# Issuing each head pair's scores behind another pair's probability product, and moving the forget gate's sum to GpSimd, in a hybrid decoder block

## Chip, cores and metric

The kernel runs on one core of a Trainium2 chip, as one launch. The metric is the device time of that launch in microseconds (us). The time before is the median of three runs.

## What is computed

The program is one decoder block on x of 512 tokens by 1024 channels, in float32:

```python
xn = rms_norm(h, norm_mix_w)
hq, hf, hi, hg, fq, fk, fv, ff, ga, gb = split(xn @ w_in)
a = hgrn2_mixer(hq, hf, hi, hg, lb)      # 4 heads of 128
b = fox_attention(fq, fk, fv, ff, fb)    # 8 heads of 64
h = h + (sigmoid(ga) * (a @ w_a) + sigmoid(gb) * (b @ w_b)) @ w_out
h = h + peer_ffn(rms_norm(h))            # 16384 experts, 128 slots a token
return rms_norm(h)
```

The change touches `fox_attention` and its order beside the rest. For each head it computes

```python
log_f = log_sigmoid(ff + fb)             # ff: 512 tokens x 8 heads
c = cumsum(log_f, axis=token)
s[t, u] = q[t] . k[u] / 8 + c[t] - c[u]  # u <= t
o = softmax(s) @ v
```

The softmax does not depend on c[t], so the kernel adds only -c[u].

## The kernel before

The launch has three stages, separated by barriers. The first, which the change touches, ends at about 386 us of the profiled span: the input projection, the HGRN2 mixer and the attention. The second has the branch, output and query projections, and the third (most of the time) the experts.

**Weights as units.** Every weight matrix is cut into units of 1024x128. A unit is loaded by a DMA of SyncE's queue (`load_unit`), split by ScalarE into a rounded high part (`split_hi`, L210) and by GpSimd into the remainder (`split_lo`, L214), and used by TensorE in 24 matmuls (`unit_product` and `passes`, L219 to L221: high by high, high by low, low by high). Splits run four units ahead of their use (`LEAD`), and loads seven (`LOAD_LEAD`).

**The order in stage one.** Each of the five engines runs a loop over the same steps n = 0 to 44, one unit of `w_in` each: forget logits of HGRN2 at 0 to 3, its queries at 4 to 7, its values at 8 to 11, the attention's values at 12 to 15, the attention's forget logits `ff` at 16 (`FF0`), its queries at 17 to 20, its keys at 21 to 24, the merge gates at 25 to 40 and the HGRN2 output gates at 41 to 44. In each step TensorE first projects the unit (`project(n)`) and then issues what that step holds of the mixers. VectorE and ScalarE take their part of the same step in program order. Which mixer work lies in which step is written out by hand:

- HGRN2 is 4 heads of 11 events, two events a step, from `HG_STEP0` = 9 on. Events 0 to 6 of a head are levels: VectorE takes differences (`pre1`), ScalarE the exponential (`hgrn_exp`), VectorE multiplies (`pre2`, L545 and L546), TensorE multiplies (`hgrn_mm`, L714), VectorE selects (`post`, L568). Event 7 is the diagonal (L718). Event 8, OFFX, has six ScalarE instructions (L396 to L401), six on VectorE (L552 to L557) and then the matmuls of L723. Event 10 is the output (L730 to L737). VectorE does `pre2` of the second event of a step inside that step.
- The attention has 4 head pairs p, each in three steps from `FX_STEP0` = 31 on. At 31+3p TensorE issues the scores (`fox_scores_mm`, L754 to L762), VectorE takes row maxima (L584), ScalarE the exponentials (`act_fox_exp`, L365) and VectorE normalizes (L592, both in `fox_norm`). At 32+3p TensorE transposes the probabilities (`fox_transposes`, L773) and ScalarE copies them out (`act_fox_trout`, L375 and L379). At 33+3p TensorE multiplies by the values into bank 7 (`fox_pv`, L783), which VectorE copies out (`fox_out`, L597) at the head of its step 34+3p. The last of a pair's eight score blocks, head 1 by query tile 1, is in bank 7 too.
- `ON_STEP` sets where the HGRN2 output norm of each head goes (ScalarE L473, TensorE L798, VectorE L655); ScalarE takes the roots of all four at step 36 (L477), and VectorE the reciprocal and scaling of each head at steps 38, 39, 41 and 42 (`ROW_STEP`, L665 and L666).
- The forget sum is VectorE's, on 8 partitions. At step 16: bias (L622), absolute value (L625), minimum with zero (L627), negation (L628). ScalarE takes exponential and logarithm at step 17 (L453 and L455). At step 18 VectorE subtracts (L631), fills ones (L632) and scans (L633). At steps 20, 22 and 24 (`C_STEPS`) it peels off one of three bfloat16 parts of the sum into rows 0, 32 and 64 of `negc3` (L637 to L639) and writes the rows of `head_row` that select a head (L641, 8 instructions). Pair 0's scores wait for all of it.

## Time and profile before

| | before |
|---|---|
| median of three runs (1795.12, 1801.9, 1802.53) | 1801.9 us |
| the profiled execution | 1790.98 us |
| its span | 1789.2 us |
| mean granted TensorE clock | 0.986 of full speed |
| TensorE busy | 1721.5 us, 96% |
| VectorE busy | 1231.1 us, 69% |
| ScalarE busy | 778.7 us, 44% |
| GpSimd busy | 776.5 us, 43% |

The span is the stretch between the first and the last instruction of one profiled execution. The engines overlap, so their busy times do not add up to it. Idle time is given in the profile in front of the instruction that ended it, with the instruction that released it.

### The profile page before, as it was taken

The page shows a single profiled execution, that of the slowest core. Times are in us where ns is not written, and L with a number is a line of the kernel's source. Part 1 is how long each engine was busy: PE and PEld are TensorE (multiplying, and loading weights), DVE is VectorE, ACT ScalarE, POOL GpSimd, SP SyncE. Part 2 cuts the span into 40 slices and gives each one's busy share as a digit, 9 for nine tenths or more (in the row PEclk, how much of TensorE's full clock was granted, in tenths as well). Part 3 has the DMA queues.
Part 4 walks back from the last instruction along what each step waited for, and adds up shares of the span by engine and source line. Part 5 has one row for each costly group of instructions (what it writes and reads, how often), then busy time and mean ns, then how long its engine had stood idle before and what let it go on. Part 6 is the DMA issues. An engine that isn't in the chain of part 4 may idle for free.

```text
span 1789.2 us, 25724 instructions
## 1 busy us (share of the span) xinstructions
PE 1721.5 (96%) x9603; PEld 1603.3 (90%) x9603; DVE 1231.1 (69%) x2306; ACT 778.7 (44%) x1367; POOL 776.5 (43%) x478
## 2 busy tenths in 40 slices
PE   6998999989999999999999999998999999999996
PEld 4786876668788999999999999998999999999996
DVE  6556633464252589999989866643888888888884
ACT  4333325444321333346677766733333333333332
POOL 4332322234333487876554567784232223232210
PEclk8999999999999999999999999999999999999998
DMA  6332232235433599987777799998999999999981
GB/s 172 92 83 56 69 107 83 77 121 168 115 114 107 179 312 298 323 303 277 251 277 254 283 321 361 376 376 319 350 350 350 363 357 351 344 371 336 356 304 48
DMA packets 260844, 436.09 MB, mean 244 GB/s; under 512 B 14960, under 2 KB 184176, under 8 KB 259056
## 3 DMA queue, kind: packets, MB, share of 16 engines
q1 hardware_dynamic: 203696, 249.87, 43.2%
q0 software_dynamic: 36864, 134.23, 19.8%
q10 hardware_dynamic: 20160, 50.34, 7.5%
q8 instruction: 77, 1.26, 0.3%
q14 instruction: 47, 0.39, 0.1%
HBM read 373.57 MB, written 60.82 MB: 243 GB/s over the span
## 4 chain that ended last, share of the span: by engine, by line
PE 47%; issue 6%; DVE 5%; POOL 5%; DMA 3%; ACT 1%; SPq 0%; DVEq 0%; POOLq 0%; ACTq 0%
PE bank L219 13%; PE bank L221 13%; PE bank L220 13%; PE x_rows L219 2%; PE x_rows L221 2%; PE x_rows L220 2%; POOL rows L1081 2%; POOL spl_a L214 2%; PE bank L1531 1%; DMA rows<-in_u_rows,expert 1%; DVE rows L1090 1%; DMA raw<-in_v_tab 1%; DMA raw<-in_u_t 1%; DVE hot L1316 0%; DVE lists L1344 0%
## 5 line engine op out<-in xcount | busy, mean ns | idle before, releaser
L214 POOL TENSOR_TENSOR spl_a<-raw,spl_a 128x1024 fp32r<-128x1024 f32 x172 | 413.5, 2406 | 394.0 <-ACT spl_a L210 393.1
L210 ACT ACTIVATE spl_a<-raw 128x1024 fp32r<-128x1024 f32 x296 | 312.9, 1059 | 401.4 <-PE bank L221 280.6
L219 PE MATMUL bank<-act,spl_a 128*128 128x384 f32 (+1 forms) x1216 | 431.3, 355 | 12.1 <-DVE act L509 7.4
L220 PE MATMUL bank<-act,spl_a 128*128 128x384 f32 (+1 forms) x1216 | 420.1, 345 | 0.0
L221 PE MATMUL bank<-act,spl_a 128*128 128x384 f32 (+1 forms) x1216 | 420.0, 345 | 0.0
L1081 POOL DMA_INDIRECT rows<-in_v_tab,expert x128 | 142.2, 1111 | 352.6 <-DVE hot L1457 339.5
L219 PE MATMUL bank<-aws,spl_a 128*128 128x384 f32 x768 | 258.3, 336 | 5.9 <-POOL spl_a L214 5.9
L220 PE MATMUL bank<-aws,spl_a 128*128 128x384 f32 x768 | 258.1, 336 | 0.0
L221 PE MATMUL bank<-aws,spl_a 128*128 128x384 f32 x768 | 258.0, 336 | 0.0
L219 PEld LDWEIGHTS bank<-act,spl_a 128*128 128x128 f32 x1216 | 230.6, 190 | 26.1 <-issue 13.7
L220 PEld LDWEIGHTS bank<-act,spl_a 128*128 128x128 f32 x1216 | 231.1, 190 | 8.5 <-issue 1.7
L221 PEld LDWEIGHTS bank<-act,spl_a 128*128 128x128 f32 x1216 | 230.3, 189 | 8.2
L214 DVE TENSOR_TENSOR spl_a<-raw,spl_a 128x1024 fp32r<-128x1024 f32 x124 | 151.9, 1225 | 96.4 <-ACT spl_a L210 96.4
L1090 DVE SCALAR_TENSOR_TENSOR rows<-rows,x_rows 128x1024 f32<-128x1024 f32 x128 | 155.0, 1215 | 76.6 <-DMA rows<-in_u_rows,expert 76.3
L1231 ACT ACTIVATE aws<-scb 128x384 fp32r<-128x384 f32 x128 | 67.2, 525 | 224.9 <-DVE scb L1438 224.5
L214 POOL TENSOR_TENSOR spl_b<-raw,spl_b 128x1024 fp32r<-128x1024 f32 x37 | 90.2, 2441 | 164.3 <-ACT spl_b L210 164.3
L1457 DVE SCALAR_TENSOR_TENSOR hot<-rows,a_row,hot 128x1024 f32<-128x1024 f32 x126 | 160.7, 1279 | 0.0
L219 PEld LDWEIGHTS bank<-aws,spl_a 128*128 128x128 f32 x768 | 144.7, 188 | 6.2 <-POOL spl_a L214 6.2
L220 PEld LDWEIGHTS bank<-aws,spl_a 128*128 128x128 f32 x768 | 144.8, 188 | 0.0
L221 PEld LDWEIGHTS bank<-aws,spl_a 128*128 128x128 f32 x768 | 144.8, 188 | 0.0
L1081 POOL DMA_INDIRECT rows<-in_u_rows,expert x128 | 123.2, 962 | 30.5 <-issue 16.5
L1266 ACT ACTIVATE hot<-hot,slot_t 128x128 f32<-128x128 f32 x384 | 119.6, 397 | 14.0 <-DVE hot L1316 11.6
(294 smaller groups left out, 2814.4 us busy)
## 6 DMA issues: line engine op xcount, KB each, us to landing
raw<-in_u_t SPq DMA_DIRECT2D x128, 512.0 KB, 4.6
raw<-in_v_tab SPq DMA_DIRECT2D x128, 512.0 KB, 8.5
gelu_ux<-gl ACTq DMA_DIRECT2D x128, 192.0 KB, 4.9
dense_gates<-mixbuf ACTq DMA_DIRECT2D x12, 2048.0 KB, 9.0
mixbuf<-dense_gates SPq DMA_DIRECT2D x32, 768.0 KB, 9.1
mixbuf<-gelu_ux SPq DMA_DIRECT2D x32, 768.0 KB, 12.2
raw<-in_w_in SPq DMA_DIRECT2D x45, 512.0 KB, 3.9
raw<-in_w_q SPq DMA_DIRECT2D x16, 512.0 KB, 3.9
```

The source lines that it names most:

```text
L210: eng.activation(spl(n, 0, slice(0, W)), raw[:, s, :], ACT.Copy).then_inc(hi_done, 1)
L214: eng.tensor_tensor(spl(n, 1, slice(0, W)), raw[:, n % RAW, :], spl(n, 0, slice(0, W)).bitcast(F32), ALU.subtract).then_inc(lo_done, 1)
L219: nc.tensor.matmul(out, w_hi, x_hi, start=first, stop=False)
L220: nc.tensor.matmul(out, w_hi, x_lo, start=False, stop=False)
L221: return nc.tensor.matmul(out, w_lo, x_hi, start=False, stop=last)
L1081: pool.indirect_dma_start(out=rows[:, g % ROWS, :], out_offset=None, in_=u_rows[:, :] if g < SLOTS else v_rows, in_offset=bass.IndirectOff ...
L1090: dve.scalar_tensor_tensor(out=row, in0=row, scalar=1.0, in1=x, op0=ALU.mult, op1=ALU.mult, accum_out=z_row[:, g:g + 1]).then_inc(row_used, 1)
L1231: act_e.activation(aws[:, 0, j % AWS, :], aw[:, j % 2, :], ACT.Copy).then_inc(a_hi, 1)
L1266: ins = act_e.activation(hot[:, q % HOTS, 1, t, :], hot[:, q % HOTS, 1, t, :], ACT.Copy, scale=slot_t[:, 2, col:col + 1])
L1457: dve.scalar_tensor_tensor(out=acc[:, s % 2, :], in0=row, scalar=a_row[:, s:s + 1], in1=acc[:, s % 2, :], op0=ALU.mult, op1=ALU.add) \
L1531: ins = nc.tensor.matmul(bank[4 + q % 2][:, t * P:(t + 1) * P], hot[:, q % HOTS, 0, t, :], hot[:, q % HOTS, 1, t, :], start=True, stop=True)
```

## The change

The HGRN2 events and the attention's steps go one step later. The scores of pairs 1, 2 and 3 are issued at steps 34, 37 and 40, the step of the previous pair's value product and right behind it; transposes are at 33, 36, 39, 42 and value products at 34, 37, 40, 43. VectorE copies a pair's product out in the product's own step, ahead of the next pair's `fox_norm`. On TensorE the wait for that copy stands only before the last of the eight blocks. The root goes to step 35, and the four scalings to 36, 36, 39 and 39.

The `ff` unit comes from a new array `w_ff`, in which the 8 columns stand three times (rows 0, 32, 64 of the result, zeros between), so the sum is made on 72 partitions. VectorE keeps the bias (step 16) and the scan (step 21). GpSimd makes the rest behind its own splits: three instructions at step 17, two at step 19, six and a no-operation at step 21, most of them followed by a wait for their own end (`link`). ScalarE's exponential and logarithm go to step 18. `head_row` comes from a new input of 72x1024 float32 (`c_head`, 295 KB) by a DMA ahead of the first unit's load and one GpSimd copy, in place of 24 VectorE copies; two GpSimd fills go.

```diff
-HG_STEP0 = 9
-FX_STEP0 = 31
+HG_STEP0 = 10
+FX_STEP0 = 32
-ROW_STEP = [38, 39, 41, 42]
-C_STEPS = [20, 22, 24]
+ROOT_STEP = 35
+ROW_STEP = [36, 36, 39, 39]
+SCORES_STEP = [FX_STEP0] + [FX_STEP0 + 3 * p - 1 for p in range(1, PAIRS_FX)]
...
                 sp.dma_start(probs[:, 0:8 * P], c_mask).then_inc(mask_in, 16)
+                sp.dma_start(probs_t[0:FR, 0:HF * P], c_head).then_inc(mask_in, 16)
...
-                pool.wait_ge(mask_in, 16)
+                pool.wait_ge(mask_in, 32)
...
+                pool.tensor_copy(head_row[:, :, :].rearrange("p h t -> p (h t)"), probs_t[0:FR, 0:HF * P]) \
+                    .then_inc(c_ready, 1)
...
                 for n in range(N_IN):
                     split_lo(pool, n + LEAD)
+                    if n == FF0 + 1:
+                        pool.wait_ge(proj_out[FF0 % 2], FF0 // 2 + 1)
+                        link(pool.tensor_scalar(negc[:, :], ff[:, 0, :], 0.0, None, ALU.min))
+                        link(pool.tensor_tensor(ff[:, 1, :], negc[:, :], ff[:, 0, :], ALU.subtract))
+                        pool.tensor_tensor(ff[:, 1, :], ff[:, 1, :], negc[:, :], ALU.add).then_inc(ff_abs, 1)
+                    if n == FF0 + 3:
+                        pool.wait_ge(ff_soft, 1)
+                        link(pool.tensor_tensor(ff[:, 0, :], negc[:, :], ff[:, 1, :], ALU.subtract))
+                        pool.memset(ff[:, 1, :], 1.0).then_inc(ff_log, 1)
+                    if n == FF0 + 5:
+                        pool.wait_ge(lo_done, n + LEAD + 1)
+                        pool.wait_ge(ff_scan, 1)
+                        link(pool.tensor_copy(negc3[:, :], negc[:, :]))
+                        link(pool.tensor_tensor(negc[:, :], negc[:, :], negc3[:, :], ALU.subtract))
+                        link(pool.tensor_copy(negc3[32:64, :], negc[32:64, :]))
+                        link(pool.tensor_copy(negc3[64:FR, :], negc[64:FR, :]))
+                        link(pool.tensor_tensor(negc[64:FR, :], negc[64:FR, :], negc3[64:FR, :], ALU.subtract))
+                        link(pool.tensor_copy(negc3[64:FR, :], negc[64:FR, :]))
+                        pool.nop(nofuse=True).then_inc(c_ready, 1)
...
                     if n == FF0:
                         dve.wait_ge(unit_used, n + 1)
-                        dve.tensor_scalar(ff[:, 0, :], pr[0:HF, :], fbias[:, 0:1], None, ALU.add) \
+                        dve.tensor_scalar(ff[:, 0, :], pr[0:FR, :], fbias[:, 0:1], None, ALU.add) \
                             .then_inc(proj_out[n % 2], 1)
-                        dve.wait_ge(proj_out[n % 2], n // 2 + 1)
-                        dve.scalar_tensor_tensor(out=ff[:, 1, :], in0=ff[:, 0, :], scalar=-1.0,
-                                                 in1=ff[:, 0, :], op0=ALU.mult, op1=ALU.max)
-                        link(dve.tensor_scalar(negc[:, :], ff[:, 0, :], 0.0, None, ALU.min))
-                        dve.tensor_scalar(ff[:, 1, :], ff[:, 1, :], -1.0, None, ALU.mult).then_inc(ff_abs, 1)
-                    if n == FF0 + 2:
-                        dve.wait_ge(ff_soft, 1)
-                        link(dve.tensor_tensor(ff[:, 0, :], negc[:, :], ff[:, 1, :], ALU.subtract))
-                        link(dve.memset(ff[:, 1, :], 1.0))
-                        link(dve.tensor_tensor_scan(negc[:, :], ff[:, 1, :], ff[:, 0, :], 0.0,
-                                                    ALU.mult, ALU.subtract))
-                    if n in C_STEPS:
...
+                    if n == FF0 + 5:
+                        dve.wait_ge(ff_log, 1)
+                        dve.tensor_tensor_scan(negc[:, :], ff[:, 1, :], ff[:, 0, :], 0.0,
+                                               ALU.mult, ALU.subtract).then_inc(ff_scan, 1)
...
-                    if part == 0 and 0 < p <= PAIRS_FX:
-                        fox_out(p - 1)
-                    if part == 0 and 0 <= p < PAIRS_FX:
-                        fox_norm(p)
+                    if part == 2 and 0 <= p < PAIRS_FX:
+                        fox_out(p)
+                    if n in SCORES_STEP:
+                        fox_norm(SCORES_STEP.index(n))
...
                     else:
                         pe.wait_ge(fx_trout, 6 * p)
-                        pe.wait_ge(fx_out, p)
                     for a in range(2):
                         for i in (3, 2, 0, 1):
+                            if p and (a, i) == (1, 1):
+                                pe.wait_ge(fx_out, p)
...
-                    if 0 <= p < PAIRS_FX:
-                        [fox_scores_mm, fox_transposes, fox_pv][part](p)
+                    if part == 1 and 0 <= p < PAIRS_FX:
+                        fox_transposes(p)
+                    if part == 2 and 0 <= p < PAIRS_FX:
+                        fox_pv(p)
+                    if n in SCORES_STEP:
+                        fox_scores_mm(SCORES_STEP.index(n))
```

## Rows read from the trace of the kernel before

**Rows 1.** The page: TensorE's busy time, and its granted clock in 40 slices.
```profile
PE 1721.5 (96%) x9603; PEld 1603.3 (90%) x9603; DVE 1231.1 (69%) x2306; ACT 778.7 (44%) x1367; POOL 776.5 (43%) x478
...
PEclk8999999999999999999999999999999999999998
```

**Rows 2.** TensorE's waits, 0 to 400 us: total us, times, longest.
```profile
PE bank L773 <- DVE s_all L592: 10.6, 4, 4.1
...
PE bank L723 <- DVE offs L557: 3.8, 1, 3.8
PE bank L714 <- DVE lev L546: 3.6, 2, 2.2
```

**Rows 3.** Windows: length, busy us of PE, PEld, DVE, ACT, POOL, then PEclk.
```profile
84.60:92.00 7.40, 7.35 (x40) 6.40 (x41) 6.92 (x14) 3.52 (x5) 3.52 (x2) 1.00 0.28 72
141.00:144.40 3.40, 3.40 (x9) 2.08 (x8) 3.13 (x8) 1.90 (x3) 0.00 (x0) 0.50 0.00 0
161.50:164.90 3.40, 3.40 (x11) 2.79 (x10) 1.56 (x4) 0.00 (x0) 0.00 (x0) 0.50 0.74 200
...
332.20:339.00 6.80, 5.95 (x24) 5.66 (x25) 6.73 (x4) 3.77 (x7) 0.64 (x1) 0.50 0.37 116
```

**Rows 4.** Timeline, steps 9 and 16: start us, us, engine, line, idle before.
```profile
84.65 2.05 PE L714 MATMUL bank<-lev 128*128 128x128 f32 x16 [1.40 <-DVE lev L546]
...
137.07 0.74 DVE L622 TENSOR_SCALAR probs<-bank,fbias 8x512 f32<-8x512 f32 x1 [3.68 <-PE bank L221]
...
137.84 0.68 DVE L625 SCALAR_TENSOR_TENSOR probs<-probs 8x512 f32<-8x512 f32 x1
...
139.23 0.41 DVE L545 TENSOR_TENSOR lev<-lev,ab 128x256 f32<-128x256 f32 x1
...
140.12 1.23 PE L714 MATMUL bank<-lev 128*128 128x128 f32 x8 [2.19 <-DVE lev L546]
```

**Rows 5.** Timeline, steps 17 and 18.
```profile
149.75 0.61 ACT L453 ACTIVATE probs<-probs 8x512 f32<-8x512 f32 x1
...
155.03 0.19 ACT L401 ACTIVATE etot<-kc 128x2 f32<-128x2 f32 x1
...
156.24 4.75 POOL L214 TENSOR_TENSOR spl_b<-raw,spl_b 128x1024 fp32r<-128x1024 f32 x2 [9.32 <-ACT spl_b L210]
...
158.70 2.37 DVE L557 TENSOR_SCALAR offs<-offs,etot 128x128 f32<-128x128 f32 x1
...
161.22 1.37 PE L723 MATMUL bank<-offs 128*128 128x128 f32 x4 [3.84 <-DVE offs L557]
```

**Rows 6.** Timeline, pairs 1 and 2 of the attention.
```profile
294.00 0.60 PE L762 MATMUL x_rows<-fk,ab 64*128 64x256 f32 x4
...
300.65 2.48 DVE L592 TENSOR_SCALAR s_all<-s_all,stat 128x256 f32<-128x256 f32 x1
...
303.18 1.09 PE L773 MATMUL bank<-cst,probs 128*128 128x128 f32 x8 [2.91 <-DVE s_all L592]
...
313.51 0.69 DVE L597 COPY ab<-x_rows 128x512 f32<-128x512 f32 x1 [10.39 <-PE x_rows L783]
...
324.01 1.28 ACT L365 ACT_TABLE_LOAD   x1 [4.13 <-DVE stat L584]
```

**Rows 7.** Groups by line, VectorE, 0 to 390 us: busy us, mean ns.
```profile
L665 DVE RECIPROCAL kc<-kc 128x512 f32<-128x512 f32 x4 | 13.4, 3344 | 0.0
```

**Rows 8.** Timeline, steps 22 and 23.
```profile
189.36 0.40 DVE L637 CAST negp<-negc 8x512 bf16<-8x512 f32 x1
...
193.91 2.23 PE L714 MATMUL bank<-lev 128*128 128x128 f32 x16
...
194.09 0.43 DVE L545 TENSOR_TENSOR lev<-lev,ab 128x256 f32<-128x256 f32 x1
```

**Rows 9.** Timeline, the start of the kernel.
```profile
11.32 1.04 POOL L328 CAST masks<-probs 128x1024 uint8<-128x1024 f32 x1 [5.93 <-DMA probs<-in_c_mask]
...
13.08 1.06 ACT L210 ACTIVATE spl_a<-raw 128x1024 fp32r<-128x1024 f32 x1 [2.81 <-DMA raw<-in_w_in]
...
16.11 0.63 ACT L412 ACTIVATE lev<-lev 128x512 f32<-128x512 f32 x1 [1.98 <-DVE lev L499]
```

More of the change, by code:

```diff
@@ L36 @@
 DHF = 64
+FR = 64 + HF
 PH = 8
@@ L53 @@
 COL_FV = [3072 + P * i for i in range(4)]
-COL_FF = [3584]
+COL_FF = [None]
 COL_FQ = [2048 + P * i for i in range(4)]
@@ L123, in spl_before, with build @@
     return max([m for m in range(max(0, n - SPL), n) if spl_slot(m) == spl_slot(n)], default=None)
-def build(nc, xT, w_in, norm_mix, lb_logits, hgrn_norm, fox_bias, w_a, w_b, w_out, norm_ffn, w_q, keys,
+def build(nc, xT, w_in, w_ff, c_head, norm_mix, lb_logits, hgrn_norm, fox_bias, w_a, w_b, w_out, norm_ffn, w_q, keys,
           u_t, u_rows, v_tab, norm_final, c_f32, c_mask, c_iota, yT):
@@ L163, in unit_source @@
         def unit_source(n):
+            if n == FF0:
+                return w_ff.rearrange("(k p) c -> p k c", p=P)
             if n < BR0:
@@ L248, in build @@
             masks = sb(ctx, "masks", [P, 8, P], mybir.dt.uint8)
-            head_row = sb(ctx, "head_row", [64 + HF, HF, P], BF16)
-            negc3 = sb(ctx, "negc3", [64 + HF, T], BF16)
+            head_row = sb(ctx, "head_row", [FR, HF, P], BF16)
+            negc3 = sb(ctx, "negc3", [FR, T], BF16)
             masked = sb(ctx, "masked", [P, 2, P], BF16)
-            negc = sb(ctx, "negc", [HF, T])
-            negp = sb(ctx, "negp", [HF, T], BF16)
+            negc = sb(ctx, "negc", [FR, T])
             probs = sb(ctx, "probs", [P, 1280])
@@ L329, in _, with link @@
                     .then_inc(pool_zero, 1)
+                pool.tensor_copy(head_row[:, :, :].rearrange("p h t -> p (h t)"), probs_t[0:FR, 0:HF * P]) \
+                    .then_inc(c_ready, 1)
                 for n in range(LEAD):
                     split_lo(pool, n)
+                steps = [0]
+                def link(ins):
+                    steps[0] += 1
+                    ins.then_inc(pchain, 1)
+                    pool.wait_ge(pchain, steps[0])
                 for n in range(N_IN):
@@ L465, in _ @@
                     p, part = divmod(n - FX_STEP0, 3)
-                    if 0 <= p < PAIRS_FX and part == 0:
-                        act_fox_exp(act_e, p)
                     if 0 <= p < PAIRS_FX and part == 1:
                         act_fox_trout(act_e, p)
+                    if n in SCORES_STEP:
+                        act_fox_exp(act_e, SCORES_STEP.index(n))
                     if n - 1 in ON_STEP:
@@ L611, in _ @@
                     if n == HI0 - 1:
-                        dve.wait_ge(pool_zero, 6)
+                        dve.wait_ge(pool_zero, 4)
                         for h in range(HH):
@@ L657, in _ @@
                     p, part = divmod(n - FX_STEP0, 3)
[L658 to L668 removed]
+                    if part == 2 and 0 <= p < PAIRS_FX:
+                        fox_out(p)
+                    if n in SCORES_STEP:
+                        fox_norm(SCORES_STEP.index(n))
+                    for h in range(HH):
+                        if ROW_STEP[h] == n:
+                            dve.wait_ge(on_root, h + 1)
+                            link(dve.reciprocal(cum[:, h, :], cum[:, h, :]))
+                            link(dve.scalar_tensor_tensor(out=ab[:, h, :], in0=ab[:, h, :],
+                                                          scalar=hnw[:, h:h + 1], in1=cum[:, h, :],
+                                                          op0=ALU.mult, op1=ALU.mult))
                     if n >= HG0:
@@ L1591 @@
     masks.append(s == t)
+    w_ff, c_head, bias = np.zeros((D, P), np.float32), np.zeros((FR, HF, P), np.float32), np.zeros((FR, 1), np.float32)
+    for r0 in (0, 32, 64):
+        w_ff[:, r0:r0 + HF] = w_in[0][:, 3584:3584 + HF]
+        bias[r0:r0 + HF, 0] = fox_f_bias[0]
+        c_head[r0:r0 + HF, :, :] = np.eye(HF)[:, :, None]
     arrays = {
@@ L1595 @@
         "w_in": c(w_in[0]),
+        "w_ff": w_ff,
+        "c_head": c_head.reshape(FR, HF * P),
         "norm_mix": c(norm_mix_w[0].reshape(KD, P).T),
@@ L1598 @@
         "hgrn_norm": c(hgrn_norm_w[0].reshape(HH, P).T),
-        "fox_bias": c(fox_f_bias[0].reshape(HF, 1)),
+        "fox_bias": bias,
         "w_a": c(w_branch_hgrn[0]),
```

29 lines of the change are left out of this document (7 added, 22 removed).

## The prediction

> **What bounds the kernel now.** I read the page first. TensorE is busy for 96% of the span at almost full clock [rows 1], so time can be won only where it is idle, runs at the lower of its two clock levels, or gets less to do. The change gives it the same matmuls: the `ff` unit stays one unit of 128 columns, and the scores' matmuls keep their 72 rows. So I list TensorE's idle places in stage one and ask of each whether the change closes it.
>
> The waits of TensorE up to 400 us name three that belong to code the change moves [rows 2]: the transposes wait for VectorE's normalization in all four pairs (10.6 us), OFFX of head 1 waits 3.8 us once, and the level matmuls wait twice (3.6 us). The windows then show what the list leaves out [rows 3]. In three places TensorE stood idle and had a stretch at the 1.2 GHz level (clock 0.50) around or behind it: 3.4 us at 141, 3.4 us at 161.5 and 6.8 us at 332.2. Work at 1.2 GHz takes twice as long, so a stretch costs half of its busy time: 1.7, 1.7 and, of the 5.95 us busy in the third, 3.0 us. Last I read the timeline at each place, to see which instruction ends the wait.
>
> **The attention's pairs.** Pair 1's scores end at 294.6 and TensorE projects one unit; the transposes start at 303.18 after 2.91 us idle [rows 6]. So TensorE has 303.18 - 2.91 - 294.6 = 5.7 us of work, one projection, to cover a chain of 303.2 - 294.6 = 8.6 us: maxima, exponentials, normalization. The last normalization takes 2.48 us because GpSimd's split runs beside it; that is in the 8.6. Behind the change two projections, 11.3 us, lie between scores and transposes of pairs 1, 2 and 3, so 2.7 us are to spare. Pair 2 has a 1.28 us table load of ScalarE in its chain [rows 6] and waits longest, 4.1 us [rows 2]; with two projections it still has 1.5 us to spare. Pair 0 keeps one projection and its wait. The four waits are 10.6 us; those of pairs 1 and 2 are 2.9 and 4.1 [rows 2, 6]. Pairs 3 and 1 have the same chain without the load, so I take 2.9 for pair 3, and 10.6 - 2.9 - 4.1 - 2.9 = 0.7 stays with pair 0. Gone: 9.9 us of waits, and the 3.0 us of the half clock at 332.2, since the wait that it belongs to goes. Together **12.9 us**.
>
> What could be late next is the block in bank 7, now written right behind the product that occupied it. VectorE's copy-out starts when the product ends and takes 0.69 us [rows 6]. Seven of eight score blocks precede it, so I take 0; if none of them covered it, it would cost 0.7 us a pair, 2.1 us in all. The copy is behind two scalings on VectorE: two reciprocals of 3.34 us [rows 7] and two short instructions, some 8.3 us. They start when normalization is over (8.6 us behind the scores, pair 2: 9.9) and end by about 18.2; the next product ends at 11.3 + 10.3 = 21.6, as pair 1's copy-out starts 313.51 - 303.18 = 10.3 us behind its transposes' start [rows 6]. A margin of some 3 us; each of the four may lose up to one split of 2.4 us to GpSimd, so at the worst the last block waits a few us.
>
> **The first HGRN2 level.** At 84.65 TensorE had waited 1.40 us for VectorE, which came late out of its scans [rows 4]. One step later a projection covers it: **1.4 us**, with no clock stretch to win (the 7.4 us from there on ran at clock 1.00) [rows 3].
>
> **The bias at step 16.** VectorE does L622, then three more instructions (137.84 to 139.23, 1.39 us), and only then the multiplications that TensorE waits for, 2.19 us [rows 4]. Only L622 stays. The wait falls by 1.4 us to 0.8. The half clock at 141 (1.7 us) followed this wait; the 1.40 us wait at 84.65 had none behind it [rows 3], and 0.8 is shorter, so I count it as gone. **3.1 us**; 1.4 if the clock falls all the same.
>
> **OFFX of head 1 at step 18.** This looks as if the sum on VectorE caused it, and it did not. ScalarE is what is late: its two instructions of the sum with two table loads stand before OFFX's exponentials, which end at 155.2 [rows 5]. Then GpSimd runs two splits back to back (156.24 to 160.99), and VectorE's last multiplication, L557, lasts 2.37 us beside the second, where one of 256 elements lasts 0.41 [rows 4, 5]. TensorE starts 0.2 us behind it. Both the sum on ScalarE and OFFX move by one step, so their order is the same. What differs is that GpSimd now has its step 19 instructions between the two splits. The second block on VectorE then lasts one subtraction of half a split's length, 4.75 / 4 = 1.2 us, in place of 2.4: the wait falls from 3.8 to 2.6, **1.2 us**. Bounds: 0 if the split still comes in between, 3.8 with the clock's 1.7 besides if the wait vanishes. I take 1.2, and leave the clock stretch at 161.5 in, since no row shows a wait of 2.6 us without one.
>
> **The added GpSimd work.** The trace has no such instructions on GpSimd. By L214 (4.75 us for two of 1024 elements) a two-input one of 512 takes 1.2; by L328 (1.04 us for 1024) a copy takes 0.5 [rows 5, 9]. Five of the first kind, six others of 0.5 to 1.2: 9 to 13 us in three bursts of about 3.5, 1.8 and 5 us. GpSimd splits four units ahead, over 22 us by four projections of 5.7, so a burst delays no projection. It can delay VectorE, whose multiplications for the next level run then. How much can VectorE bear? At step 22 the old sum held it for 194.09 - 189.36 = 4.7 us, and 16 level matmuls took 2.23 us instead of the 2.05 at 84.65 [rows 4, 8]: 0.2 us lost, which is now won back. The new bursts, up to 5 us long, should cost about as much or a little more, 0.3; the balance is **-0.1**, and up to 3 us lost if they add to a split just then. Behind the waiting GpSimd queue stand only splits, which have these 22 us.
>
> The Trainium skill, "SBUF — State Buffer", section "Who interferes with whom", says that VectorE and GpSimd share a pair of ports as a lock held for a whole instruction, and that a VectorE instruction with two inputs in SBUF contends when GpSimd reads there. The 2.48 us of L592 beside a split agrees [rows 6]. By that rule alone one could charge the whole added GpSimd time, 9 to 13 us, to VectorE; with what VectorE is seen to bear, it changes the sum by less than 1 us. "GPSIMD Engine Reference", section "Elementwise — side-by-side cycle accounting", gives 4497 ns for 2048 elements, an estimate of 1.1 us for 512, and the sum would be the same by it.
>
> **The start.** `c_head` adds 295 KB ahead of unit 0. ScalarE's split of unit 0 ends at 14.1, and what it does next starts at 16.11, when VectorE lets it [rows 9]: 2 us of cover. The mask load, 512 KB, is the nearest thing; at its pace the addition is under 2 us. I take 0; 0 to 1.5 lost. The GpSimd copy (1 us) precedes a split that TensorE needs only when the norm, whose root starts at 16.1, has been applied. Bias rows 72 in place of 8, and two fills gone: nothing waits for them. The end of stage one, two projections and the gating of head 3, is as it was.
>
> **Sum.** 12.9 + 1.4 + 3.1 + 1.2 - 0.1 = 18.5 us off the profiled span: 1789.2 becomes about 1771, and the profiled execution's 1790.98 about 1772.5. The median of the runs lies 10.9 above that execution, and nothing in it hints that they differ in stage one, so the median becomes 1801.9 - 18.5 = 1783.4; I say **1783**. Later stages start earlier and are otherwise the same: their loads run only seven units ahead, so they shift as a whole.
>
> **Rivals.**
> - OFFX's wait ends too: GpSimd's instructions are short enough for VectorE to slip through, 2.6 + 1.7 us more, so 1779. For it: the second split causes half of the wait. Against: ScalarE is late by itself. 0.15.
> - The pairs' waits return as a wait for the copy-out in bank 7, behind the scalings. Three waits of up to 2 to 3 us, with a fall of the clock at one of them: 6 to 10 us back, 1789 to 1793. For it: VectorE is in order, and its margin is one split. Against: 3 us of margin in a chain of known durations. 0.13.
> - The saving doesn't reach the end: the 7 us between the three runs shows something outside stage one that absorbs or adds as much. 1797 to 1802. Nothing in the trace speaks for it. 0.06.
> - Slower: GpSimd's unseen forms (a minimum, copies that start at partition 32 or 64) take far longer than rows say. VectorE bears 4 to 5 us a burst; beyond that each us stops TensorE. The eleven would have to last about 14 + 18.5 + 9 = 41 us, 3.8 us each instead of 0.5 to 1.2, for a loss of over 0.5%. 1811 and up. 0.04.
> - The forecast, 0.62.
>
> **Range.** 1773 to 1794: the forecast's own is 1779 to 1790 by the bounds (2.6 + 1.7 better; 1.7 + 3 + 1.5 worse), and the first two rivals and the runs' own spread take it to the ends. 0.5% is 9 us, about what a measurement of this kernel tells from no change. Faster by more: 0.62 + 0.15 + 0.11 = 0.88; within: 0.08; slower: 0.04.
>
> **What would show it.** Right: no idle before L773 but for one of 0.7 us; no clock stretch in the attention; waits of about 0.8 us for the levels at step 16 and 2.6 us before the OFFX matmuls of head 1; scores of pairs 1 to 3 starting right behind L783. Wrong: an idle place inside the score blocks released by L597, level matmuls waiting at steps 17 to 22 beside GpSimd instructions on `negc`, or a first projection that starts later than before.

## The result, and the profile after

| | before | after |
|---|---|---|
| median of the runs (six each) | 1795.23 us (1790.51 to 1802.53) | 1774.31 us (1771.80 to 1776.36) |
| ratio, with its 95% interval | | 0.988 (0.9852 to 0.9907) |
| the profiled execution, and its span | 1790.98, 1789.2 us | 1773.98, 1772.1 us |
| first projection starts | 22.45 us | 22.09 us |
| second stage's first matmul | 389.66 us | 369.28 us |
| from the one to the other | 367.2 us | 347.2 us |

The kernel is faster, by 20.9 us or 1.2% on the medians. The forecast was 1783 us, with a range of 1773 to 1794. Three more runs of the kernel before brought its median from 1801.9 down to 1795.2 us; why it moves so far is told below.

First the page, section one and the clock, of the kernel after. It answers to [rows 1]:

```profile
PE 1718.7 (97%) x9603; PEld 1603.5 (90%) x9603; DVE 1219.9 (69%) x2268; ACT 778.3 (44%) x1367; POOL 782.9 (44%) x488
...
PEclk8999999999999999999999999999999999999998
```

TensorE has the same 9603 matmuls, 38 VectorE instructions are gone, and GpSimd has ten more. The page doesn't show where 17 us of span went. TensorE's waits up to 400 us do; they answer to [rows 2] (total us, times, longest):

```profile
PE bank L739 <- DVE offs L589: 2.7, 1, 2.7
...
PE bank L746 <- DVE s_all L606: 1.2, 2, 0.6
PE bank L790 <- DVE s_all L624: 0.7, 1, 0.7
PE bank L730 <- DVE lev L578: 0.7, 1, 0.7
```

The transposes (L773, now L790) wait 0.7 us in all instead of 10.6, and only for pair 0. The levels (L714, now L730) wait once, 0.7 us, instead of 1.4 and 2.2. OFFX of head 1 (L723, now L739) waits 2.7 us instead of 3.8. Nothing in the list is new. The windows, which answer to [rows 3], show the clock around these places and in pair 1:

```profile
134.00:138.00 4.00, 3.30 (x19) 2.88 (x19) 3.89 (x10) 1.12 (x2) 0.00 (x0) 1.00 0.47 131
157.00:160.30 3.30, 0.62 (x6) 0.44 (x5) 3.30 (x3) 1.31 (x2) 3.24 (x3) 1.00 0.09 11
160.60:164.00 3.40, 3.40 (x11) 2.75 (x10) 1.71 (x4) 0.00 (x0) 2.39 (x2) 0.50 0.44 130
286.50:300.00 13.50, 13.50 (x72) 10.84 (x70) 11.85 (x20) 10.96 (x26) 3.62 (x2) 1.00 0.19 41
```

Behind the short wait of step 16 the clock stays at 1.00. Behind OFFX it falls to 0.50 for 3.4 us as before. In pair 1, from the end of the scores through two projections into the transposes, TensorE is busy all the time. The timeline of pair 1:

```profile
283.81 0.69 DVE L629 COPY ab<-x_rows 128x512 f32<-128x512 f32 x1 [7.08 <-PE x_rows L800]
...
287.20 0.60 PE L779 MATMUL x_rows<-fk,ab 64*128 64x256 f32 x4
...
293.86 2.55 DVE L624 TENSOR_SCALAR s_all<-s_all,stat 128x256 f32<-128x256 f32 x1
...
298.89 1.03 PE L790 MATMUL bank<-cst,probs 128*128 128x128 f32 x8
```

Scores end at 287.8, normalization at 296.4, and the transposes start at 298.9 with no idle time in front. The chain is 8.6 us long, as in [rows 6]; it has 11.1 us of cover now. Step 16 and OFFX answer to [rows 4] and [rows 5]:

```profile
133.21 0.75 DVE L654 TENSOR_SCALAR probs<-bank,fbias 72x512 f32<-72x512 f32 x1 [3.71 <-PE bank L225]
133.87 0.41 DVE L577 TENSOR_TENSOR lev<-lev,ab 128x256 f32<-128x256 f32 x1
...
134.76 0.68 PE L730 MATMUL bank<-lev 128*128 128x128 f32 x4 [0.70 <-DVE lev L578]
```

```profile
156.49 2.38 POOL L218 TENSOR_TENSOR spl_b<-raw,spl_b 128x1024 fp32r<-128x1024 f32 x1 [6.96 <-ACT spl_b L214]
...
156.70 2.26 DVE L588 TENSOR_SCALAR offs<-offs,etot 128x128 f32<-128x128 f32 x1
...
158.83 1.26 POOL L354 TENSOR_TENSOR probs<-negc,probs 72x512 f32<-72x512 f32 x1
158.88 1.30 DVE L589 TENSOR_SCALAR offs<-offs,etot 128x128 f32<-128x128 f32 x1
...
160.32 0.90 PE L739 MATMUL bank<-offs 128*128 128x128 f32 x3 [2.70 <-DVE offs L589]
```

L589 waits for the short GpSimd subtraction (1.26 us) instead of a second split of 2.4 us. That is the difference between 3.8 and 2.7 us; `e3_gpsimd_later` below undoes it alone.

### The profile page after: what moved, and what is told of

Read it like the earlier page. It is cut to its first block, busy times and chain, and to the rows that moved or that the text cites. A ratio compares the mean times of both kernels' runs of the same rounds, so it can differ in the third digit from the quotient of the medians.

```text
span 1772.1 us, 25695 instructions
## 1 busy us (share of the span) xinstructions
PE 1718.7 (97%) x9603; PEld 1603.5 (90%) x9603; DVE 1219.9 (69%) x2268; ACT 778.3 (44%) x1367; POOL 782.9 (44%) x488
## 3 DMA queue, kind: packets, MB, share of 16 engines
q8 instruction: 77, 1.26, 0.3%
## 4 chain that ended last, share of the span: by engine, by line
PE 48%; issue 6%; DVE 5%; POOL 5%; DMA 2%; ACT 1%; SPq 0%; DVEq 0%; POOLq 0%; ACTq 0%
PE bank L223 13%; PE bank L225 13%; PE bank L224 13%; PE x_rows L223 3%; PE x_rows L224 3%; PE x_rows L225 3%; POOL rows L1102 2%; POOL spl_a L218 2%; PE bank L1552 1%; DVE rows L1111 1%; DMA rows<-in_u_rows,expert 1%; DMA raw<-in_u_t 1%; DMA raw<-in_v_tab 1%; DVE hot L1337 1%; DVE lists L1365 0%
## 5 line engine op out<-in xcount | busy, mean ns | idle before, releaser
L1102 POOL DMA_INDIRECT rows<-in_v_tab,expert x128 | 134.8, 1053 | 363.4 <-DVE hot L1478 349.8
L1287 ACT ACTIVATE hot<-hot,slot_t 128x128 f32<-128x128 f32 x384 | 119.7, 397 | 14.0 <-DVE hot L1337 11.1
```

Of the source, the lines that this page charges most:

```text
L1102: pool.indirect_dma_start(out=rows[:, g % ROWS, :], out_offset=None, in_=u_rows[:, :] if g < SLOTS else v_rows, in_offset=bass.IndirectOff ...
L1287: ins = act_e.activation(hot[:, q % HOTS, 1, t, :], hot[:, q % HOTS, 1, t, :], ACT.Copy, scale=slot_t[:, 2, col:col + 1])
```

## The experiments

Whole times of one kernel lie up to 14 us apart here, so most runs are read by a stretch within the profile: from the first projection's start to the second stage's first matmul. It leaves out the start, which moved between 20.8 and 23.0 us over fourteen profiles, and the last stage, whose pitch (the time from one matmul's start to the next) is not the same in all profiles. A half clock is a stretch at granted clock 0.50. In some runs one falls behind the first projection (near 33 us), in kernels with the change and without; it is in the stretch and costs 1.7 us. Where a run has one, the table says so. Every profile also has one at its start, of which 3.9 to 6.2 us of TensorE's work lie in the stretch (1.9 to 3.1 us lost), so two single profiles that differ by less than about 1 us here are not told apart by their stretches alone. One that begins in the 3.9 us of idle time in front of the second stage costs nothing and is left out of the table.

| run | stretch, us | waits of TensorE, us | half clock, us from the start |
|---|---|---|---|
| before | 367.2 | 1.4, 2.2, 3.8; 0.7, 2.9, 4.1, 2.9 | 141 and 161.5 (3.4 each), 332.2 (6.8) |
| after | 347.2 | 0.7, 2.7; 0.7 | 160.6 (3.4) |
| `e1_pairs_only` | 353.3 | 1.4, 2.2, 3.8; 0.7 | 140.1, 160.6 (3.4 each) |
| `e2_shift_only` | 371.6 | 2.2, 5.5, 1.0; 0.7, 2.8, 4.1, 4.2 | 33.4, 309.8, 340.6, 371.3 (3.4 each), 156.2 (6.8) |
| `e3_gpsimd_later` | 349.5 | 0.7, 3.8; 0.7 | 161.5 (6.8) |
| `e4_bias_thrice` | 350.1 | 2.0, 2.7; 0.7 | 137.2, 164.5 (3.4 each) |
| `e5_log_later` | 342.7 | 0.7; 0.7 | none |
| `e6_no_shift` | 345.8 | 1.4, 0.7; 0.7 | 33.5 (3.4) |
| `e7_copyout_first` | 351.7 | 0.7, 2.7; 0.7; copy-out 0.9, 0.95, 0.95 | 33.8, 163.5 (3.4 each) |
| `e8_gpsimd_double` | 353.1 | 0.7, 2.7, 1.9, 2.0; 0.7 | 162.3, 189.6 (3.4 each) |
| `e9_both_fixes` | 341.7 | 0.7 | none |
| `a1_changed_again` | 345.7 | 0.7, 2.7; 0.7 | none |
| `b1_before_again` | 368.9 | as before | 32.0, 141.3, 161.8, 332.4, 363.1 (3.4 each) |
| `b2_before_again` | 369.8 | as before | 33.1, 302.7 (3.4 each), 159.4, 333.4 (6.8 each) |

(Waits of the mixers alone, to 0.1 us, in order of time, those of the transposes behind the semicolon. Every run has two more of 0.6 us in front of the output event of heads 1 and 3.)

**The order of the pairs alone** (`e1_pairs_only`). Edit of the kernel before:

```diff
-ROW_STEP = [38, 39, 41, 42]
+ROW_STEP = [35, 35, 38, 38]
+ROOT_STEP = 34
...
+SCORES_STEP = [FX_STEP0] + [FX_STEP0 + 3 * p - 1 for p in range(1, PAIRS_FX)]
...
-                    if 0 <= p < PAIRS_FX:
-                        [fox_scores_mm, fox_transposes, fox_pv][part](p)
+                    if part == 1 and 0 <= p < PAIRS_FX:
+                        fox_transposes(p)
+                    if part == 2 and 0 <= p < PAIRS_FX:
+                        fox_pv(p)
+                    if n in SCORES_STEP:
+                        fox_scores_mm(SCORES_STEP.index(n))
```

with ScalarE, VectorE and the wait for the copy-out as in the change. Expected:

> The kernel before with the new order of the pairs alone: scores at steps 31, 33, 36 and 39, roots at 34, scalings at 35, 35, 38 and 38; HGRN2 and the forget sum as before. My theory: the order of the pairs alone removes three of the four waits of the transposes (9.9 us) and the half clock at 332 (3 us), 12.9 us in all; the waits of 1.4 us (first level), 2.2 us (step 16) and 3.8 us (OFFX of head 1) and the two other half clock stretches stay. The second stage then starts 12.9 us earlier than before, at 376.8 instead of 389.7, and the median falls by 11 to 15 us. Rival: the waits shrink because GpSimd and VectorE are relieved elsewhere, or come back as a wait for the copy-out of bank 7; then this kernel gains under 8 us, and a wait released by L597 stands in the score blocks.

Measured: 353.3 us, 13.9 less than before, and 1786.17 us against 1798.84 in runs beside it, ratio 0.9922 (0.9894 to 0.9951). TensorE's waits of this run:

```profile
PE bank L725 <- DVE offs L559: 3.8, 1, 3.8
PE bank L716 <- DVE lev L548: 3.6, 2, 2.2
...
PE bank L776 <- DVE s_all L594: 0.7, 1, 0.7
```

The two upper rows are those of [rows 2]; only the third has changed, from 10.6 to 0.7. Of the 13.9 us, 9.9 are idle time and 3.3 half clock; the other 0.7 us lie in TensorE's busy time at full clock and were not taken apart. So the order of the pairs is worth 13.9 of the 20.0 us by itself, and no wait for L597 took its place.

**The shift by one step alone** (`e2_shift_only`). Edit of the kernel before:

```diff
-HG_STEP0 = 9
-FX_STEP0 = 31
+HG_STEP0 = 10
+FX_STEP0 = 32
...
-ROW_STEP = [38, 39, 41, 42]
+ROW_STEP = [39, 40, 42, 43]
...
-                    if n == 36:
+                    if n == 37:
```

> The kernel before with HGRN2 and the attention one step later and nothing else (the scalings at 39, 40, 42 and 43); the sum stays on VectorE. My theory: the wait for the first level goes (1.4 us). The waits of the transposes stay (10.6 us), and so do the 2.2 us at step 16, with its half clock. OFFX of head 1 then has its exponentials one step behind ScalarE's logarithm, so its wait of 3.8 us goes with its half clock (1.7 us), though VectorE still makes the whole sum: 1.4 + 3.8 + 1.7 = 6.9 us, second stage at 382.8. Rival: the sum on VectorE causes the wait at OFFX; then it stays, here or at the levels of step 18, the gain is 1.4 us and the second stage starts at 388.3.

Measured: 371.6 us, or 369.9 without the half clock at 33: 2.7 us more than before, where 6.9 less was expected. The waits for the first level and for OFFX did go, but a new one of 5.5 us stands before the second level of step 18 (1.0 us at 192.9 and 1.3 us more before pair 3's transposes are new too and were not followed up). The timeline of this run at steps 17 and 18:

```profile
146.43 0.63 ACT L455 ACTIVATE probs<-probs 8x512 f32<-8x512 f32 x1
147.08 1.28 ACT L389 ACT_TABLE_LOAD   x1
148.38 0.63 ACT L389 ACTIVATE lev<-lev 128x512 f32<-128x512 f32 x1
...
150.51 0.63 ACT L389 ACTIVATE lev<-lev 128x512 f32<-128x512 f32 x1 [1.50 <-DVE lev L532]
...
151.02 0.67 DVE L631 TENSOR_TENSOR probs<-negc,probs 8x512 f32<-8x512 f32 x1
...
152.17 2.35 POOL L214 TENSOR_TENSOR spl_b<-raw,spl_b 128x1024 fp32r<-128x1024 f32 x1 [7.46 <-ACT spl_b L210]
...
152.37 3.23 DVE L633 TENSOR_TENSOR_SCAN negc<-probs 8x512 f32<-8x512 f32 x1
...
155.63 2.39 DVE L545 TENSOR_TENSOR lev<-lev,ab 128x256 f32<-128x256 f32 x1
```

ScalarE's logarithm and two table loads now stand before the exponentials of two levels, but the second of these is over at 151.1, and TensorE is done with the step's first level only at 153.0. What comes in between is VectorE's share of the sum, from 151.0 to 155.6: its scan lasts 3.23 us beside a split instead of 1.2, and the multiplication behind it 2.39 instead of 0.4. My theory was wrong for this kernel, and the rival half right: with the shift, the sum on VectorE does cost TensorE's time, only at another place. The parts of the change don't add up. The shift alone loses; what it is worth with the sum off VectorE, `e5_log_later` and `e6_no_shift` show.

**GpSimd's two instructions one step later** (`e3_gpsimd_later`). Edit of the changed kernel:

```diff
-                    if n == FF0 + 3:
+                    if n == FF0 + 4:
                         pool.wait_ge(ff_soft, 1)
```

> The changed kernel with GpSimd's two instructions of step 19 at step 20, so that GpSimd's two splits stand back to back again while VectorE multiplies for OFFX. My theory: VectorE's last multiplication (L589, 1.30 us in the changed kernel, 2.37 before) waits for a whole split again, and the wait before OFFX's matmuls goes from 2.7 back to 3.8 us. Second stage 1.1 us later than in the changed kernel. Rival: the wait is ScalarE's alone; then it stays at 2.7 us.

The timeline of this run before L739:

```profile
157.43 2.38 POOL L218 TENSOR_TENSOR spl_b<-raw,spl_b 128x1024 fp32r<-128x1024 f32 x1 [6.96 <-ACT spl_b L214]
...
159.76 2.34 POOL L218 TENSOR_TENSOR spl_a<-raw,spl_a 128x1024 fp32r<-128x1024 f32 x1
159.81 2.38 DVE L589 TENSOR_SCALAR offs<-offs,etot 128x128 f32<-128x128 f32 x1
```

Measured: L589 lasts 2.38 us beside the second split, the wait before L739 is 3.8 us again, and a half clock of 6.8 us in place of 3.4 comes with it. The stretch is 2.3 us longer, 1.1 of it the wait. My theory holds: what VectorE is held by here is the GpSimd instruction that runs beside it, whole. And the wait is the 3.8 us of before with nothing of the sum on VectorE in that step, so the old sum on VectorE had no part in it.

**VectorE's step 16 as long as before** (`e4_bias_thrice`).

```diff
                         dve.wait_ge(unit_used, n + 1)
+                        dve.wait_ge(c_ready, 1)
+                        for r in range(2):
+                            dve.tensor_scalar(probs_t[0:FR, r * T:(r + 1) * T], pr[0:FR, :], fbias[:, 0:1],
+                                              None, ALU.add)
                         dve.tensor_scalar(ff[:, 0, :], pr[0:FR, :], fbias[:, 0:1], None, ALU.add) \
```

> The changed kernel with two more VectorE instructions like the bias (72x512 from the bank, results unused) ahead of it, 0.74 us each, so 1.5 us more of VectorE at step 16, as much as the removed three took. My theory: the wait at step 16 goes from 0.7 to 2.2 us and the TensorE clock falls to 0.5 behind it for 3.4 us, as before: 1.5 + 1.7 = 3.2 us. Rival: the clock's fall at that place hung on something else in the kernel before; then 1.5 us and no half clock near 136 us.

Measured: 350.1 us, 2.9 more than the changed kernel, where 3.2 was expected. The wait is 2.0 us, and behind it the clock is at 0.50, as in the kernel before; the window of this run:

```profile
137.20:140.60 3.40, 3.40 (x12) 2.82 (x12) 3.23 (x8) 1.87 (x4) 0.00 (x0) 0.50 0.00 0
```

**The logarithm one step later** (`e5_log_later`). The profile after named a version to try: at step 19 ScalarE has no exponentials of HGRN2 (events 18 and 19 give it none two events ahead), so the sum's logarithm fits there.

```diff
-                    if n == FF0 + 2:
+                    if n == FF0 + 3:
                         act_e.wait_ge(ff_abs, 1)
...
-                    if n == FF0 + 3:
+                    if n == FF0 + 4:
                         pool.wait_ge(ff_soft, 1)
...
-                    if n == FF0 + 5:
+                    if n == FF0 + 6:
                         dve.wait_ge(ff_log, 1)
```

and GpSimd's last block at `FF0 + 6` too.

> The changed kernel with ScalarE's exponential and logarithm of the sum at step 19 in place of 18, where ScalarE has no exponentials of HGRN2, and what follows them one step later (GpSimd's subtraction at 20, scan at 21 + 1 = 22, the three parts at 22). My theory: OFFX's exponentials of head 1 then come in time, its wait of 2.7 us and the half clock of 3.4 us behind it go, 4.4 us in all, and nothing new waits. Counted from the first projection, the second stage starts at 342.8 instead of 347.2. Rival: as in the run that only shifted, a late logarithm makes VectorE late for its levels; then a wait of several us appears at L730 in steps 19 to 22 and the gain is under 2 us.

Measured: 342.7 us, 4.5 less than the changed kernel (0.7 of it from the half clock at the start, which is shorter in this profile). No wait before L739, and over the whole place the clock is full, as the window of this run shows:

```profile
145.00:175.00 30.00, 29.39 (x156) 24.79 (x155) 14.92 (x30) 13.79 (x22) 13.12 (x7) 1.00 0.26 67
```

**No shift** (`e6_no_shift`).

```diff
-HG_STEP0 = 10
-FX_STEP0 = 32
+HG_STEP0 = 9
+FX_STEP0 = 31
...
-ROOT_STEP = 35
-ROW_STEP = [36, 36, 39, 39]
+ROOT_STEP = 34
+ROW_STEP = [35, 35, 38, 38]
```

> The changed kernel without the shift by one step (HGRN2 from step 9, attention from 31; roots at 34, scalings at 35 and 38). My theory: the wait of 1.4 us for the first level returns; the one before OFFX of head 1 goes with its half clock (2.7 + 1.7 us), since its exponentials are now a step ahead of the logarithm. 3.0 us better than the changed kernel: 344.2 from the first projection to the second stage. Rival: the shift is what the changed kernel's gain at these places comes from; then both waits of the kernel before are back (1.4 and 3.8) and it is 2 to 3 us worse.

Measured: 345.8 us, 344.1 without the half clock at 33.5, as expected. So in the changed kernel the shift trades a wait of 1.4 us for one of 2.7 us and its half clock: with the logarithm where the change puts it, the shift costs 3 us by these waits. Only with the logarithm moved on does the shift pay: `e5_log_later`, which has both, is at 342.7 us, 1.4 less than these 344.1.

**The wait for the copy-out ahead of all eight blocks** (`e7_copyout_first`).

```diff
                         pe.wait_ge(fx_trout, 6 * p)
+                        pe.wait_ge(fx_out, p)
                     for a in range(2):
                         for i in (3, 2, 0, 1):
-                            if p and (a, i) == (1, 1):
-                                pe.wait_ge(fx_out, p)
```

> The changed kernel with TensorE's wait for the copy-out of bank 7 ahead of all eight score blocks of pairs 1 to 3. My theory: the copy takes 0.7 us and nothing else holds VectorE then, so 0.7 to 0.8 us at each of three places, 2.2 us in all, against nothing in the changed kernel. Rival: the scalings ahead of the copy in VectorE's order are still running; then more than 1.5 us at a place, and the changed kernel was near its margin.

From TensorE's waits of this run (total us, times, longest):

```profile
PE bank L770 <- DVE ab L629: 2.8, 3, 1.0
```

Measured: three waits of 0.9 to 1.0 us, 2.8 in all. Without the half clock at 33.8 the stretch is 350.0, also 2.8 more. The wait is what the copy takes and no more; the scalings are long over. In the changed kernel VectorE stood idle 3.0 to 3.1 us before each of the copies of pairs 1 and 2.

**GpSimd's burst three times as long** (`e8_gpsimd_double`).

```diff
+                        for r in range(8):
+                            link(pool.tensor_tensor(probs_t[0:FR, 0:T], negc[:, :], ff[:, 0, :], ALU.subtract))
                         link(pool.tensor_copy(negc3[:, :], negc[:, :]))
```

> The changed kernel with eight more GpSimd subtractions of 72x512 at step 21 (each 1.2 us, with a wait for its end; results unused), so that its burst there grows from 5 to some 15 us. My theory: GpSimd takes turns with VectorE at every instruction, and VectorE has about 4 us to spare in a step: TensorE waits 2 to 6 us in steps 21 to 23, and no projection waits for a split. Rival A: a link leaves VectorE room enough, and nothing waits. Rival B: the splits behind the burst come late and a projection waits for L218.

Two timelines of this run at step 21, GpSimd's and then VectorE's:

```profile
178.41 11.18 POOL L360 TENSOR_TENSOR probs_t<-negc,probs 72x512 f32<-72x512 f32 x8
```

```profile
180.04 1.29 DVE L579 TENSOR_TENSOR lev<-lev,ab 128x256 f32<-128x256 f32 x1
181.25 1.51 DVE L580 TENSOR_TENSOR lev<-lev,kc 128x256 f32<-128x256 f32 x1
182.68 1.51 DVE L565 TENSOR_TENSOR lev<-kc 128x256 f32<-128x256 f32 x1
184.12 1.51 DVE L566 TENSOR_TENSOR lev<-kc 128x256 f32<-128x256 f32 x1
```

Measured: 353.1 us, 5.9 more: two waits of 1.9 and 2.0 us before the levels and a half clock between them. The two engines take turns at every instruction, VectorE's 0.4 us becoming 1.5. GpSimd's splits come late without holding up a projection; but two of them, pushed to 195.4 to 200.3 us, run beside two VectorE multiplications that take 2.64 and 2.56 us, just before the second wait. So the eight subtractions (11.2 us from the first to the last) cost TensorE 3.9 us of waits; the change's own burst of some 5 us costs it nothing that the profile shows.

**Both edits, and the changed kernel beside it** (`e9_both_fixes`, `a1_changed_again`). `e9_both_fixes` has the edit of `e5_log_later` and

```diff
                     elif n == FF0:
-                        pass
+                        act_e.activation(ff[:, 0, :], pr[0:FR, :], ACT.Identity, bias=fbias[:, 0:1]) \
+                            .then_inc(proj_out[n % 2], 1)
...
-                    if n == FF0:
-                        dve.wait_ge(unit_used, n + 1)
-                        dve.tensor_scalar(ff[:, 0, :], pr[0:FR, :], fbias[:, 0:1], None, ALU.add) \
-                            .then_inc(proj_out[n % 2], 1)
```

> The version with the logarithm at step 19, and besides it the bias of the sum made by ScalarE (an Identity with bias out of the bank, step 16, where it has no other copy to make) in place of VectorE. My theory: the wait of 0.7 us at step 16 goes too, since VectorE has nothing of the sum there. From the first projection to the second stage 342.0 us, against 342.7 with the first edit alone, 347.2 in the changed kernel and 367.2 before; the median 25 to 26 us below before and 5 below the changed kernel, if the executions fall on the same levels of the last stage's pitch. Rival: ScalarE's 0.6 us delays the exponentials of step 16 and the wait stays at 0.7.

> The changed kernel as it is, once more, beside the version above and on the same chip. My theory of the saving says that stage one is 20 us shorter from the first projection on, in any execution: 347 us in this profile again, with 0.7, 2.7 and 0.7 us of waits at steps 16, 19 and 33. The three levels of TensorE's pitch in the last stage (4.16, 4.19 and 4.24 us a unit, 10 us from the lowest to the highest over 128 units) belong to the execution and not to the kernel, so this profile may show any of them. Rival: the pitch is a property of the built kernel; then it is 4.19 again.

Measured: 341.7 us and no wait at step 16. By whole times `e9_both_fixes` is 1770.04 us, ratio 0.9866 to before (0.9845 to 0.9887), and the changed kernel beside it 1772.05 us, 0.9877 (0.9854 to 0.9899). It beats the kernel before clearly; over the changed kernel its gain is seen in the profile (4 to 5.5 us of stage one) and not resolved by the whole times. Its median is 22.6 us below before and 2.0 below the changed kernel, less than the 25 to 26 and 5 expected, though both profiles are at the same pitch; why is open. The changed kernel's second profile has the same waits as its first and 345.7 us instead of 347.2: the clock did not fall behind the 2.7 us wait this time, as the window behind it shows.

```profile
161.00:164.40 3.40, 3.40 (x18) 2.87 (x18) 2.42 (x4) 0.00 (x0) 2.46 (x2) 1.00 0.47 138
```

**The kernel before, twice more** (`b1_before_again`, `b2_before_again`).

> The kernel before as it is, profiled again, to tell whether TensorE's pitch in the last stage is the execution's or the kernel's. Its first profile shows 4.16 us a unit and 1791.0 us. My theory: the pitch belongs to the execution; in one of two more profiles it is 4.19 or 4.24, with a time about 4 or 10 us higher at the same length of stage one (367 us from the first projection). Rival: it is fixed by the built kernel; then 4.16 in both, and times within 2 us of 1791.

> As the run before it: the kernel before once more. My theory: any of the three levels of pitch, and the profiled time follows it. Rival: 4.16 us a unit again.

Windows of 450 us in the last stage, where TensorE has no idle time: of the kernel before in its first profile, then of the changed one, then of `b1_before_again`, one fence each (behind the length: TensorE's busy us and, in brackets, its matmuls).

```profile
1250.00:1700.00 450.00, 450.00 (x2598) 450.00 (x2597) 368.94 (x439) 171.96 (x217) 127.26 (x113) 1.00 0.99 353
```

```profile
1250.00:1700.00 450.00, 450.00 (x2578) 450.00 (x2577) 366.43 (x436) 170.55 (x215) 118.81 (x112) 1.00 0.99 350
```

```profile
1250.00:1700.00 450.00, 450.00 (x2549) 450.00 (x2549) 362.12 (x432) 168.25 (x212) 117.78 (x111) 1.00 0.98 347
```

At full clock and without a gap, the same matmuls come 173.2, 174.6 or 176.5 ns apart (450 us by the count). The last stage's second half has 3072 of them: 4 us from the first level to the second and 10 us to the third. `b1_before_again` (1801.16 us) and `b2_before_again` (1804.84 us) are both at the third level, though the built kernel is the one that showed the first: the built kernel alone does not set the level. Nor does the chip: `e1_pairs_only` (third level), `e2_shift_only` and `e3_gpsimd_later` (second) and `e4_bias_thrice` (first) ran on one chip. No kernel was profiled at two levels on one chip, so a level that kernel and chip set together is not excluded. Against it speak the seven whole times of `e1_pairs_only` on its chip, 1780.3 to 1781.3 us in three and 1786.2 to 1786.9 in four, as far apart as the second and the third level; the pitch in those without a profile was not seen. The time from the second stage's first matmul to the end follows the levels in all fourteen profiles: 1399.5 to 1399.8 us, 1402.9 to 1405.3 and 1409.6 to 1412.0. Their stretches are 368.9 and 369.8 us, 1.7 and 2.6 more than in the first profile. The waits are the same; the stretches of half clock differ, as the table has them: both runs have one of 3.4 us (1.7 us lost) behind the first projection, which the first profile has not.

## Why the prediction was right, point by point

**The pairs, 12.9 us: right, a little small.** Alone they are worth 13.9 us. The chain of 8.6 us, the cover of two projections, pair 2's spare time in spite of its table load, and the 0.7 us left to pair 0 are all as worked out. Of the 1 us more, 0.3 is half clock, most of it at the start of the profile, and 0.7 TensorE's busy time; the latter stays open.

**The copy-out in bank 7, 0 us: right.** Seven blocks cover it. Moving the wait ahead of them costs 2.8 us, somewhat above the 2.1 given as the bound, since each wait is the copy's 0.7 us with some 0.2 us around it (for pair 1, 0.05 from the product's end to the copy and 0.15 from the copy's end to TensorE).

**The first level, 1.4 us: right** as a term. But it is the shift that buys it, and the shift moved OFFX's exponentials onto the step of the logarithm, to which the change had moved it too.

**The bias at step 16, 3.1 us: right.** The wait fell from 2.2 to 0.7 us, and the half clock behind it vanished; putting the time back on VectorE brought back both (2.9 us).

**OFFX, 1.2 us: right, and by the mechanism told.** 3.8 to 2.7 us, by a GpSimd instruction of 1.26 us in place of one of 2.4. That the old sum on VectorE had no part in it, as the prediction says, `e3_gpsimd_later` shows. One line was wrong in its ground: that the clock's fall would stay, "since no row shows a wait of 2.6 us without one". [rows 6] shows such a wait, the 2.91 us of pair 1, and none of the half clocks of [rows 3] lies behind it. The fall did stay in the profile after, and not in the second one, with the same wait; that the term came out is in part luck.

**The added GpSimd work, -0.1 us: right.** By the rows it came to 9 to 13 us in three bursts. Measured: 1.50, 1.53 and 1.36 us at step 17, 1.26 and 0.52 at step 19, and 0.61, 1.16, 0.68, 0.69, 1.22 and 0.69 at step 21: 11.2 us. The minimum, a one-input form, took 1.50 us, above the 1.2 given for it, and 1.49 to 1.50 in all nine profiles that have it, so this is its own length and not what VectorE made of it. The rule of the Trainium skill, "SBUF — State Buffer", "Who interferes with whom", agrees with the trace in form: L564 lasted 1.52 us instead of 0.42 beside the subtraction behind the minimum, and in `e8_gpsimd_double`, beside the eight subtractions, the VectorE instructions with two inputs took 1.29 to 1.51 us each but for one of 0.73. L592, which the prediction sets beside the rule, has one tensor input and a scalar; it shows an instruction held beside a whole split, not the case of two inputs. What it costs the kernel is what VectorE has to spare, and that only rows tell.

**The start, 0 us: right for the profile after, too low for others.** The first projection started at 22.09 us instead of 22.45, but that hides a cost. ScalarE splits unit 0 and then takes the norm's root. In the five profiles without `c_head` the split is over at 13.5 to 14.1 us and the root starts 0.03 to 0.04 us behind VectorE's sum for it. In the nine with `c_head` unit 0 arrives later, the split ends at 15.5 to 16.8 us, and the root waits for it. In `a1_changed_again` VectorE's sum was ready at 15.10 and the root starts at 16.20:

```profile
14.41 0.69 DVE L531 TENSOR_SCALAR lev<-bank 128x512 f32<-128x512 f32 x1 [3.52 <-PE bank L697]
...
15.24 1.06 ACT L214 ACTIVATE spl_a<-raw 128x1024 fp32r<-128x1024 f32 x1 [5.45 <-DMA raw<-in_w_in]
16.20 0.61 ACT L444 ACTIVATE lev<-lev 128x512 f32<-128x512 f32 x1
```

TensorE's idle time in front of the first projection is 7.10 us in all five without `c_head`, and 7.14 to 8.95 in the nine with it: 0.04 us lost in the profile after, 1.05 in `a1_changed_again`, 1.85 in `e8_gpsimd_double`, 0.7 on average. The term that was off is the 2 us of cover: the split's end moved by 1.4 to 2.6 us against the 14.1 of before, and in the profile after the cover was just used up. The bound of 1.5 was a little too low. No run undid this part alone.

**The sum and the median.** 18.5 us were forecast for the span; stage one became 20.0 us shorter from the first projection on, and the medians differ by 20.9. The forecast of 1783 was 8.7 us too high. Of that, 6.7 us is the step "the median becomes 1801.9 - 18.5": two of the three runs shown were near 1802 us, and three more brought the median down to 1795.2. The 1774.3 measured lies outside the 1779 to 1790 that the prediction calls the forecast's own and 1.3 us inside its full range, in the part kept for a rival that did not come true and for the runs' spread; that the whole time fell inside is in part luck. The one profile, at the fastest level of pitch, could not tell that the last stage alone moves a run by up to 10 us. The span fell by only 17.1 us although the second stage began 20.4 us earlier: from its first matmul to the end it is 1402.9 us instead of 1399.5, since the two profiles were at different levels of pitch (4 us by the count of matmuls); two later profiles of the kernel before have 1409.6 and 1412.0 us there. The rival "the saving doesn't reach the end" is thereby refuted; it reaches it, under a spread that it was right to suspect.

**The rivals.** That OFFX's wait would end, with VectorE slipping through between GpSimd's instructions, was wrong; it ends in `e5_log_later`, but because the logarithm moves. That the pairs' waits return at bank 7 was refuted by the profile. That GpSimd's forms are slow was refuted: 0.52 to 1.53 us each.

## What to carry to other kernels

Where a chain over several engines is longer than the work that covers it, move its start ahead and not its end: one more projection between the scores and their transposes removed three of four waits, while none of the instructions became faster. When work moves to another engine, look for what else runs in the step that it lands in: the same logarithm costs TensorE a wait of 2.7 us, and mostly 1.7 us of half clock behind it, in one step, and nothing in the next. And compare executions by a stretch of the profile that holds the change; whole times here carry up to 10 us that belong to the last stage's pitch.

## What the runs showed of the hardware

- **TensorE's pitch in a long stretch of equal matmuls has levels.** At granted clock 1.00 and with no idle time, the 128x384 matmuls come every 173.2, 174.6 or 176.5 ns for over 500 us on end. Over the fourteen profiles of this study the three levels occur three, seven and four times. The kernel before showed the first and the third, and one chip all three. What sets them is open.
- **The clock's fall behind a wait is not certain.** Behind the same wait of 2.7 us before OFFX it fell in four profiles and not in `a1_changed_again`; behind a wait of 1.7 us near 33 us, which all fourteen profiles have, it fell in five; in the kernel before, a wait of 2.9 us had none behind it in the first profile, and in `b1_before_again` a stretch of 3.4 us began at 363.1, behind such a wait. What decides it is open.
- **VectorE and GpSimd alternate instruction by instruction** when both have work that contends: 1.51, 1.51, 1.51 us for VectorE instructions of 0.42, beside GpSimd subtractions of 1.27 to 1.36 us (`e8_gpsimd_double`).
